# Expert rows of the second layer: from a selection product on TensorE to rows in HBM and an indirect fetch

## What is computed

```python
combine = jnp.sum(jax.nn.one_hot(expert_ids, N_EXPERTS, dtype=jnp.float32)
                  * w_sel[..., None], axis=1)
hid = (jax.nn.silu(jnp.einsum("nd,edf->nef", t, w_gate))
       * jnp.einsum("nd,edf->nef", t, w_up))
y = jnp.einsum("nef,efd->nd", hid * combine[:, :, None].astype(hid.dtype), w_down)
```

## Time and profile before

| | |
|---|---|
| median of 3 runs | 547.8 us (547.42 to 549.92) |
| the profiled execution | 546.32 us |
| its span | 544.5 us |
| TensorE products | 528.7 us busy, 97% |
| VectorE | 299.2 us, 55% |
| ScalarE | 219.5 us, 40% |
| GpSimd | 18.7 us, 3% |
| DMA | 189.77 MB, mean 349 GB/s |
| HBM written | 1.06 MB |
| chain that ended last | TensorE 83%, VectorE 9%, ScalarE 3%, DMA 2% |

### The profile page before, as it was taken

The page is one execution under the profiler, slowest core; times in us unless marked ns, Lnnn a source line. Parts: engine busy times, 40 slices in busy tenths (PEclk is TensorE's granted clock), DMA queues, the critical chain, the costliest instruction groups (busy, mean ns, idle before and its releaser), DMA issues.

```text
span 544.5 us, 8078 instructions
## 1 busy us (share of the span) xinstructions
PE 528.7 (97%) x3236; PEld 346.8 (64%) x3236; DVE 299.2 (55%) x502; ACT 219.5 (40%) x384; POOL 18.7 (3%) x76
## 2 busy tenths in 40 slices
PE   7799999999999999999999999999999999999996
PEld 6468968868756444444357998986876544444433
DVE  3628985799872122212369489589988112222233
ACT  2518555552445222222258265654245431222221
POOL 3104100000000000000000000000000000000000
PEclk9999999999999999999999999999999999999999
DMA  8999999979669999999999944965966999999972
GB/s 298 387 387 363 400 399 415 421 309 422 246 251 414 413 414 411 413 412 417 415 386 387 401 162 131 397 255 200 409 242 252 321 335 415 415 414 413 413 303 81
DMA packets 52222, 189.77 MB, mean 349 GB/s; under 512 B 4722, under 2 KB 4818, under 8 KB 44884
## 3 DMA queue, kind: packets, MB, share of 16 engines
q1 hardware_dynamic: 50784, 185.62, 87.5%
q0 software_dynamic: 1072, 2.45, 1.3%
q10 hardware_dynamic: 324, 1.13, 0.6%
HBM read 188.12 MB, written 1.06 MB: 347 GB/s over the span
## 4 chain that ended last, share of the span: by engine, by line
PE 83%; DVE 9%; ACT 3%; DMA 2%; issue 1%; SPq 1%; ACTq 0%; DVEq 0%
PE ps L1790 20%; PE ps L1547 13%; PE ps L1816 10%; PE ps L1668 8%; PE ps L1554 7%; PE ps L1770 5%; PE ps L1832 5%; PE ps L1414 4%; DMA raw<-in_w_ada_dram 2%; DVE wlo L856 2%; DVE cbc L1103 1%; PE ps L1406 1%; SPq L356 1%; PE ps L1449 1%; DVE stat L1073 1%
## 5 line engine op out<-in xcount | busy, mean ns | idle before, releaser
L856 DVE TENSOR_TENSOR wlo<-raw,whi 128x1024 fp32r<-128x1024 f32 x64 | 75.7, 1220 | 16.3 <-ACT whi L551 16.0
L551 ACT ACTIVATE whi<-raw 128x1024 fp32r<-128x1024 f32 x64 | 65.4, 1057 | 24.7 <-PE ps L1547 14.3
L1816 PE MATMUL ps<-raw,work 128*64 128x512 f32 x256 | 57.8, 593 | 0.0
L1790 PE MATMUL ps<-raw,cbc 128*64 128x512 f32 x256 | 57.0, 595 | 0.4 <-ACT work L801 0.4
L1790 PE MATMUL ps<-raw,qkT 128*64 128x512 f32 x256 | 57.1, 596 | 0.0
L1547 PE MATMUL ps<-act_hi,whi 128*128 128x256 f32 x192 | 55.0, 286 | 0.0
L1547 PE MATMUL ps<-act_hi,wlo 128*128 128x256 f32 x192 | 54.3, 283 | 0.0
L1547 PE MATMUL ps<-act_lo,whi 128*128 128x256 f32 x192 | 54.3, 283 | 0.0
L1328 DVE SCALAR_TENSOR_TENSOR work<-ps,cw,work 128x256 f32<-128x256 f32 x16 | 10.8, 674 | 76.8 <-ACT work L795 76.8
L1320 DVE TENSOR_TENSOR wlo<-v_sb,whi 128x512 fp32r<-128x512 f32 x32 | 21.0, 689 | 51.6 <-ACT whi L785 51.2
L1816 PEld LDWEIGHTS ps<-raw,work 128*64 128x64 f32 x256 | 18.2, 137 | 36.1 <-issue 35.4
(11 more groups left out here) (267 smaller groups left out, 894.9 us busy)
## 6 DMA issues: line engine op xcount, KB each, us to landing
raw<-in_w_ada_dram SPq DMA_DIRECT2D x40, 1024.0 KB, 10.6
raw<-in_w_gate_dram SPq DMA_DIRECT2D x64, 512.0 KB, 9.9
raw<-in_w_up_dram SPq DMA_DIRECT2D x64, 512.0 KB, 11.1
raw<-in_w_down_dram SPq DMA_DIRECT2D x32, 1024.0 KB, 11.9
raw<-in_w_in_dram SPq DMA_DIRECT2D x23, 1024.0 KB, 14.5
raw<-in_w_ada_dram SPq DMA_DIRECT2D x16, 512.0 KB, 11.5
raw<-in_w_out_dram SPq DMA_DIRECT2D x8, 1024.0 KB, 6.0
res<-in_x_dram ACTq DMA_DIRECT2D x1, 1024.0 KB, 5.0
```

Of the source, the lines that this page charges most:

```text
L551: act.activation(whi[:, slot(n), :], raw[:, r, (i % 2) * 1024:(i % 2 + 1) * 1024], ACT.Copy).then_inc(hi_done, 1)
L856: dve.tensor_tensor(wlo[:, slot(n), :], raw[:, ring_slot[("w", l, i // 2)], (i % 2) * 1024:(i % 2 + 1) * 1024], whi[:, slot(n), :].bitcast ...
L1790: ins = pe.matmul(ps[i * SLOTS:(i + 1) * SLOTS, 0, :], hg[p // 2 % 2][:, k, c0:c0 + SLOTS], ws[i][:, :, kk, :], start=(k == 0), stop=(k == ...
L1816: ins = pe.matmul(ps[i * SLOTS:(i + 1) * SLOTS, 2 + n, :], hidT[:, p % 2, kk, i * SLOTS:(i + 1) * SLOTS], ws[i][:, c0:c0 + 512], start=(kk ...
```

## The change

In layer 1 (`ROW_LAYERS`) the first six pairs (`ROW_PAIRS`) no longer take part in scatter. Their y_f goes to an HBM tensor `y_rows`, 128 rows of 4 KB per pair, by a DMA that ScalarE issues. One row more holds zeros. VectorE makes from `slot_of` and the one-hot rows of the first and second expert an index per token, row_i: the row of its y, or the row of zeros where the expert is one of the last four (or the token has no place). When all six are written, GpSimd fetches one row per token by an indirect DMA into tokmaj, for both tiles of 128 tokens, adds them to `res`, and does the same for the second expert. VectorE waits for these additions ahead of its own last ones. Pairs 6 and 7 are as before.

```diff
+        row_base = slots[:, SLOTS:SLOTS + 2 * ROW_PAIRS]
+        row_f = slots[:, P - 2 * T:P]
+        row_i = sb("row_i", [P, 2 * T], I32)
...
+        NO_ROW = ROW_PAIRS * P
+        y_rows = nc.dram_tensor("y_rows", [len(ROW_LAYERS), NO_ROW + 1, D], F32).ap()
...
+            def fetch_rows(l):
+
+                n = row_layer(l)
+                pool.wait_ge(no_row_out, 16 * len(ROW_LAYERS))
+                pool.wait_ge(row_known, n + 1)
+                pool.wait_ge(y_out, 16 * ROW_PAIRS * (n + 1))
+                for c in range(2):
+                    if c > 0:
+                        pool.wait_ge(rows_added, T * (2 * n + c))
+                    for t in range(T):
+                        pool.indirect_dma_start(tokmaj[:, t, :], None, y_rows[n, :, :],
+                                                bass.IndirectOffsetOnAxis(ap=row_i[:, T * c + t:T * c + t + 1], axis=0)
+                                                ).then_inc(rows_in, 16)
+                    pool.wait_ge(rows_in, 16 * T * (2 * n + c + 1))
+                    for t in range(T):
+                        pool.tensor_tensor(res[:, t, :], res[:, t, :], tokmaj[:, t, :], ALU.add
+                                           ).then_inc(rows_added, 1)
...
+            for n in range(len(ROW_LAYERS)):
+                pool.dma_start(y_rows[n, NO_ROW, :].rearrange("(p f) -> p f", f=8), r_w[:, 0, 0, NR:NR + 8]
+                               ).then_inc(no_row_out, 16)
             pool.wait_ge(par_in, 16 * NPAR)
...
+            if L - 1 in ROW_LAYERS:
+                fetch_rows(L - 1)
...
                 def y_high(p):
+                    if p < first_part(l):
+                        act.wait_ge(yg_ready, 2 * (NP * l + p) + 2)
+                        act.dma_start(y_rows[row_layer(l), p * P:(p + 1) * P, :], y_f).then_inc(y_out, 16)
+                        return
...
                 dve.tensor_copy(over_i[:, l:l + 1], over[:, NE:NE + 1]).then_inc(over_known, 1)
+                if l in ROW_LAYERS:
+                    es = slice(0, 2 * ROW_PAIRS)
+                    row = rnk[:, :, es]
+                    dve.wait_ge(row_base_ready, 1)
+                    link(dve.tensor_tensor(row, slot_of[:, :, es],
+                                           row_base.unsqueeze(1).to_broadcast([P, T, 2 * ROW_PAIRS]), ALU.add))
+                    link(dve.scalar_tensor_tensor(out=row, in0=slot_of[:, :, es], scalar=float(SLOTS), in1=row,
+                                                  op0=ALU.is_lt, op1=ALU.mult))
+                    dve.tensor_tensor(pick[:, 0, :, es], oh1[:, :, es], row, ALU.mult)
+                    link(dve.tensor_tensor(pick[:, 1, :, es], oh2[:, :, es], row, ALU.mult))
+                    link(dve.tensor_reduce(row_f.rearrange("p (c t) -> p c t", c=2), pick[:, :, :, es],
+                                           AX.X, ALU.add))
+                    link(dve.tensor_scalar(row_f, row_f, float(NO_ROW), None, ALU.add))
+                    dve.tensor_copy(row_i[:, :], row_f).then_inc(row_known, 1)
...
-                        if p > 0:
-                            dve.wait_ge(ylo_ready, 2 * (NP * l + p - 1) + n + 1)
+                        if p > first_part(l):
+                            dve.wait_ge(ylo_ready, 2 * parts_before(l, p - 1) + n + 1)
+                        elif p > 0:
+                            dve.wait_ge(y_out, 16 * (ROW_PAIRS * row_layer(l) + p))
...
+                    if p < first_part(l):
+                        return
...
+                if l in ROW_LAYERS:
+                    dve.wait_ge(rows_added, 2 * T * (row_layer(l) + 1))
                 dve.wait_ge(over_known, l + 1)
...
-                sel_transposes(range(0, NP // 2))
+                sel_transposes(range(first_part(l), NP // 2))
...
-                        sel_transposes(range(NP // 2, NP))
+                        sel_transposes(range(max(first_part(l), NP // 2), NP))
                     hid_transpose(p)
-                    if p >= 2:
+                    if p - 2 >= first_part(l):
                         scatter(p - 2)
...
-                scatter(NP - 3, (0,))
+                if NP - 3 >= first_part(l):
+                    scatter(NP - 3, (0,))
                 hid_transpose(NP - 1)
-                scatter(NP - 3, (1,))
+                if NP - 3 >= first_part(l):
+                    scatter(NP - 3, (1,))
```

More of the change, by code:

```diff
@@ L27 @@
 SLOTS = 64
+ROW_PAIRS = 6
+ROW_LAYERS = (1,)
 PAIR_BANK = (0, 2, 0, 2)
@@ L262, in trunk @@
         scatter_done = sem("scatter_done")
+        y_out = sem("y_out")
+        no_row_out = sem("no_row_out")
+        row_base_ready = sem("row_base_ready")
+        row_known = sem("row_known")
+        rows_in = sem("rows_in")
+        rows_added = sem("rows_added")
         moe_added = sem("moe_added")
@@ L281, in trunk, with first_part, parts_before, scatters_before @@
         X_LOADS = 16 * 5 * NE
+        def first_part(l):
+            return ROW_PAIRS if l in ROW_LAYERS else 0
+        def parts_before(l, p):
+            return sum(NP - first_part(i) for i in range(l)) + p - first_part(l)
+        def scatters_before(l):
+            return sum(NP - first_part(i) + 1 for i in range(l))
+        def selT_before(l):
+            return sum((NP - first_part(i)) // 2 for i in range(l))
+        def row_layer(l):
+            return sum(1 for i in ROW_LAYERS if i < l)
         chunks = [("A0", 0), ("A1", 0)]
@@ L502, in _ @@
                                ).then_inc(gate_full, 16)
+                if l in ROW_LAYERS:
+                    fetch_rows(l)
             for g, kind in enumerate(("G1", "G2")):
@@ L547, in split_half @@
                 if l > 0 and i < RING and slot(n) < 3:
-                    act.wait_ge(scatter_done, (NP + 1) * l)
+                    act.wait_ge(scatter_done, scatters_before(l))
                 elif l > 0 and i == 2:
-                    act.wait_ge(scatter_done, (NP + 1) * l - 2)
+                    act.wait_ge(scatter_done, scatters_before(l) - 2)
                 act.activation(whi[:, slot(n), :], raw[:, r, (i % 2) * 1024:(i % 2 + 1) * 1024], ACT.Copy
@@ L769, in selT_out @@
                 def selT_out(a):
-                    act.wait_ge(selT_done, 4 * l + a + 1)
+                    act.wait_ge(selT_done, selT_before(l) + a - first_part(l) // 2 + 1)
                     act.activation(selT[:, 4 * a:4 * a + 4, :],
@@ L773, in selT_out @@
                                    ).then_inc(selT_ready, 1)
-                selT_out(0)
-                selT_out(1)
+                if l not in ROW_LAYERS:
+                    selT_out(0)
+                    selT_out(1)
                 def y_high(p):
+                    if p < first_part(l):
+                        act.wait_ge(yg_ready, 2 * (NP * l + p) + 2)
+                        act.dma_start(y_rows[row_layer(l), p * P:(p + 1) * P, :], y_f).then_inc(y_out, 16)
+                        return
                     for n in range(2):
                         act.wait_ge(yg_ready, 2 * (NP * l + p) + n + 1)
-                        if n == 0 and p > 0 and p != NP - 2:
-                            act.wait_ge(scatter_done, (NP + 1) * l + p - int(p == NP - 1))
+                        if n == 0 and p > 0 and p != NP - 2 and l not in ROW_LAYERS:
+                            act.wait_ge(scatter_done, scatters_before(l) + p - int(p == NP - 1))
                         cols = slice(n * 512, (n + 1) * 512)
@@ L805, in _ @@
                     if p == 0:
-                        selT_out(2)
+                        if l not in ROW_LAYERS:
+                            selT_out(2)
                         selT_out(3)
@@ L904, in _ @@
             dve.wait_ge(const_ready, 5)
-            dve.tensor_copy(slots[:, :], slots_i)
+            link(dve.tensor_copy(slots[:, :], slots_i))
+            dve.tensor_scalar(row_base, slots[:, 0:2 * ROW_PAIRS], float(SLOTS), -float(NO_ROW), ALU.mult, ALU.add
+                              ).then_inc(row_base_ready, 1)
             dve.tensor_tensor(r_sum[:, :], ident[:, 0:NR], ident[:, 32:32 + NR], ALU.add).then_inc(rsum_ready, 1)
@@ L1315, in y_parts @@
                                           ).then_inc(yg_ready, 1)
+                    if p < first_part(l):
+                        return
                     for n in range(2):
-                        dve.wait_ge(yhi_ready, 2 * (NP * l + p) + n + 1)
+                        dve.wait_ge(yhi_ready, 2 * parts_before(l, p) + n + 1)
                         cols = slice(n * 512, (n + 1) * 512)
@@ L1340, in moe_row @@
                 def moe_row(t):
-                    dve.wait_ge(scatter_done, (NP + 1) * l + (NP + t if l + 1 < L else NP + 1 + 2 * t))
+                    dve.wait_ge(scatter_done, scatters_before(l) + NP - first_part(l) + (t if l + 1 < L else 1 + 2 * t))
                     row = res[:, t, :].rearrange("p (a b) -> p a b", a=2)
@@ L1345, in last_half_row @@
                 def last_half_row(t, n):
```

(12 more changed lines are left out.)

## The result

| | before | changed |
|---|---|---|
| median | 548.86 us (4 runs, 547.42 to 551.36) | 567.23 us (4 runs, 565.26 to 568.51) |
| profiled span | 544.5 | 565.8 |
| TensorE products, count | 528.7 us, 3236 | 527.2 us, 3176 |
| GpSimd busy | 18.7 | 32.0 |
| DMA | 189.77 MB | 195.01 MB |

The change is slower: ratio 1.0333, 95% interval 1.0299 to 1.0366, or 18.4 us. Of the spans' difference, 21.3 us, 1.7 were there before the experts of layer 1 began (the first gate product starts at 422.39, before at 420.66); against that 420.66 the other profiles lie 0.5 to 4.2 us later too, those of the two kernels that keep all scatters 0.8 and 1.3.

What follows compares the result with a forecast made beforehand. TensorE was taken to pace the kernel, with the saturated weight stream close behind. GpSimd's chain would delay VectorE's additions from 537.8 to 551.5, 13.7 us; 547.8 + 13.7 = 561.5 us, range 552 to 572.

Steps and rivals of the forecast that it cites:

- TensorE's saving is void: Layer 1: TensorE loses 11.5 us of work, but the weights cannot follow; at most some 4 us could reach the end.
- the lead of 4.0: Last down blocks of layer 1: landing at 527.7, used at 531.68, so weights were 4.0 us ahead of use.
- A write costs the engines what a read does: Six 512 KB y writes before the last weights: 1.27 us of the DMA engines each, 7.6 us in all.
- TensorE would wait from pair 3 or 4, 3.7 us a pair: Layer 1 expert pairs: TensorE 12.8 us against DMA 16.5, so the lead shrinks by 3.7 a pair until TensorE waits.
- They are worth nothing, as that wait remains: First 8 selection transposes ahead of the combine product: removal gains nothing, as the product waits for VectorE's weights until 425.40.
- Start of GpSimd's chain, 523: Sixth y write in layer 1: issued at 518, landing 5 us later, so fetch_rows starts at 523.
- TensorE's side, 544.4: End of layer 1: last down product at 538.3 instead of 531.68, TensorE side ready for VectorE's additions at 544.4.
- Round one, 11 us, additions 4.8, round two 7.9, additions 4.8: GpSimd's fetch_rows: first rows in at 534, added by 538.8, second rows in at 546.7, added by 551.5.
- rival 3: GpSimd's fetches: slow indirect issues, 3 us more each, or scattered rows landing late, +12 us, 567 to 580; chance 0.17.
- The tail behind the chain is the same: After VectorE's last additions start, at 551.5 instead of 537.8: the remaining time to the end is unchanged.
- The wait for the last y write is covered: VectorE's y_parts: its wait, 5 us after the write's issue, ends long before the next down product, a pair later.
- Rival 5, the clock: TensorE in layer 1: waits in each pair could drop its clock to 1.2 GHz, about 605 us; dear kind chance 0.04.

Runs made afterwards that it cites:

- the two kernels that keep all scatters: Kernel before with 8 layer-1 selection transposes moved behind the combine product, 550.12 us; kernel before with six unread y writes added, 555.43 us.
- the two bare runs: Changed kernel without y writes, fetches and GpSimd's additions: 547.85 us; the same with the first 8 layer-1 selection transposes put back: 546.35 us.
- the run with four pairs: Changed kernel with ROW_PAIRS 4 instead of 6 and the 8 selection transposes kept, fetch in two rounds as in the change: 557.66 us, ratio 1.0157.
- the split additions: Changed kernel with second fetch issued right behind the first, GpSimd adding the first round, VectorE the second, 8 transposes kept: 559.46 us, ratio 1.0195.
- the moved transposes: Kernel before with the 8 first selection transposes of layer 1 moved from ahead of the combine product to behind it: 550.12 us, ratio 1.0024.
- the transposes put back: Changed kernel with the first 8 selection transposes of layer 1 put back on TensorE, result unused: 566.01 us against 567.23.
- both fetches at once: Changed kernel with the second fetch round into its own tile, issued right behind the first; GpSimd's four additions in the same order: 563.01 us.
- the kernel before with the writes: Kernel before with all scatters kept and six y writes to HBM added that nobody reads: 555.43 us against 549.35, ratio 1.0134.

## Why the prediction was right, and where it was short

The side, the cause and the order of the two losses were as forecast: 561.5 us in 552 to 572, measured 567.23 (the kernel before at 548.86 in the same runs, so 18.4 us more where 13.7 were forecast). That the forecast isn't further off is in part luck. GpSimd's chain started 8.4 us late and ended 8.2 late; its length was met, 28.2 us for 28.5, as the first round's 1.2 us too much and the second's 1.1 too little cancel; and the end of the kernel behind VectorE's additions came out 1.5 us shorter than before. Point by point:

- **TensorE's saving is void.** Right. Of the 11.5 us the two bare runs show 1.0 and 2.0, within the lead of 4.0. That lead took the median landing of two blocks, 14.6 us. They landed 13.5 and 15.6 us after issues at 513.07 and 513.4, so the later one at about 529.0, only 2.6 us ahead of its use.
- **A write costs the engines what a read does.** Right in kind, 1.39 us instead of 1.27. For a fetched tile the sums above give about the same in the run with four pairs and less with the split additions.
- **TensorE would wait from pair 3 or 4, 3.7 us a pair.** The first wait for down weights is that of pair 4, ahead of the product at 503.55. The waits are shorter, 0.7 to 2.4 us. A gate product waits too (0.9), and there are other gaps: TensorE's gather now waits for ScalarE's copies, 3.8 us in all in five waits, as no scatter stands between. They are hidden here behind the stream.
- **"They are worth nothing, as that wait remains"**, of the first 8 transposes. This left the clock out. The wait remained, but TensorE was idle in it, and in four of five profiles the clock fell. In the changed kernel that product took 6.35 instead of 3.65, so slots came free late and the saturated stream began late: the down loads issued at 438.08 before went out at 443.19, 5.1 us later, 1.7 of them the shift of that execution. The medians give 1 us or so at most: 1.3 in the change and 0.9 in the bare runs, each taken against its own kernel before and neither clear of noise. The 1.2 of the moved transposes is what moving 1.1 us of TensorE's work behind its wait gives without any clock.
- **Start of GpSimd's chain, 523.** It was 531.45: 6.4 us late at the issue of the sixth write (524.44 instead of 518) and 7.0 instead of 5 for its landing. Of the 6.4, 5.1 had been there at 443.19 already; the rest, dearer writes among it, is by subtraction. I had taken the landing time of a transfer in a free stretch for one that stands beside a full stream; all six took 7.5 in the median. This was the term most mis-sized.
- **TensorE's side, 544.4.** It came later too, 551.2. The last down product started at 543.33 instead of 538.3, 1.7 of it the shift and 3.4 the late stream, and then took 5.35 us at the low clock instead of 3.65.
- **Round one, 11 us, additions 4.8, round two 7.9, additions 4.8.** Measured 12.2, 4.7, 6.8 and 4.6 us. An indirect issue takes 1.0 us and 0.3 between two, so rival 3 is out. A GpSimd addition takes 2.34:

```profile
L520 POOL TENSOR_TENSOR res<-res,tokmaj 128x1024 f32<-128x1024 f32 x4 | 9.3, 2344 | 13.2 <-DMA tokmaj<-y_rows,row_i 13.2
L515 POOL DMA_INDIRECT tokmaj<-y_rows,row_i x4 | 4.0, 997 | 105.2 <-DMA y_rows<-v_sb 104.3 <-issue 0.6 <-POOL res L520 0.3
```

  That is between my 2.4 and the 2.25 estimated from the GPSIMD Engine Reference of the Trainium skill (section 3.1, 4497 ns for 2048 columns); both were nearer than the bounds of 1.6 and 3.2, and the trace's 2.34 bears the page out within 4%.
- **The tail behind the chain is the same.** Not quite. VectorE reads the overflow flag and branches after its wait for GpSimd, 0.9 us (559.69 to 560.58) that lay hidden before. The output then took 5.2 us instead of 6.7 from the first addition. The four output DMAs landed in 2.1 to 2.3 us, before in 2.5 to 3.8; why is open. It isn't that no addition waits for a scatter: the same holds with both fetches at once and with split additions, and there it took 6.8 and 6.5 us.
- **The wait for the last y write is covered.** True of the change. With both fetches at once and in the kernel before with the writes VectorE's gate multiplication did wait for the sixth write, 6.8 and 5.5 us, in neither case on the path: the last gate product waited for its own weights.
- **Rival 5, the clock.** It fell in single products after waits, 5.2 to 5.35 us instead of 3.65 at three down products (pairs 4, 6 and 7), and never for long; the dear kind didn't come. Not each wait did it: with the transposes put back, waits of 2.5, 2.3 and 2.2 us for down weights (pairs 4, 5 and 6) were followed by products of 3.65, and one of 1.9 by a product of 5.25. TensorE: Matmul & The Clock Gate of the Trainium skill (HAM oscillation) tells of a kernel with DMA waits of about 3 to 5 us between short groups of products, whose clock drops each time. This case doesn't test that, as its waits for weights were 2.5 us at most.

What stays open: why a given wait drops the clock and the next doesn't, and what the low clock in the last down product costs by itself; it wasn't tried apart.

## What to carry to other kernels

A busy share of 97% says who is at work, not what the work is worth. Before taking work from the busiest engine, compare per tile its time with the bytes over the rate at which the DMA engines run full (here 14.6 against 15.2 us), and look how far ahead of their use the last loads land: that lead (2.6 us for the later block; 1 to 2 us arrived) is about the most one can win, and what the change moves in the same stretch is paid for, here 1.0 to 1.4 us for 512 KB. Work that fills a wait in front of a product may be keeping TensorE's clock up (not shown in the medians here); where it is taken out, look at the granted clock and at the next products.

## What the runs showed that was not expected

- An idle time of 1.2 us on TensorE was followed in four of five profiles by a granted clock of 0.57 to 0.74 in the 6 us from 430, and gate products of 5.35 to 6.48 us for 3.65; where transposes of 1.1 us filled it, in none of six.
- A GpSimd addition and a VectorE subtraction hinder each other; it was seen in two kernels, wherever the two fell together, and not tried by itself. With both fetches at once VectorE's two subtractions took 3.75 us instead of 1.48, and GpSimd's pair of additions 5.41 instead of 4.66. With four pairs they took 3.45 instead of 1.29, and 5.25. Nearly all of it is one subtraction, 2.84 us instead of 0.69 in both kernels. VectorE's gate multiplication, which reads PSUM, kept its 0.69 beside a GpSimd addition (546.00, changed kernel). Timelines of VectorE, both fetches at once and then four pairs:

```profile
547.65 3.75 DVE L1409 TENSOR_TENSOR wlo<-v_sb,whi 128x512 fp32r<-128x512 f32 x2
...
509.83 3.45 DVE L1403 TENSOR_TENSOR wlo<-v_sb,whi 128x512 fp32r<-128x512 f32 x2 [4.35 <-ACT whi L848]
```

- A write of 512 KB beside a full stream landed 7.5 us after its issue in the median of six, and lengthened the kernel by only 1.4.
